# Modulation panels moved in a three-part block kernel, gated heads between output gate tiles, and two norms from one pass

## What is computed

```python
mod = silu(c) @ w_mod + b_mod                      # six vectors of 1024
h   = rmsnorm(x, g_mix) * (1 + mod[1]) + mod[0]
p   = h @ w_in                                     # forget gates, values, q, og, u, v, ga, gb
o_a = rmsnorm(hgrn2(p), g_norm_a) * silu(og)       # gated recurrence, both directions, from ctx states
o_b = gelu(u) * (w_s @ layernorm(gelu(v)) + b_s)   # spatial gate
x   = x + mod[2] * ((sigmoid(ga) * (o_a @ w_pa) + sigmoid(gb) * (o_b @ w_pb)) @ w_o)
x   = x + mod[5] * swiglu(rmsnorm(x, g_ffn) * (1 + mod[4]) + mod[3], w_up, w_down)
x   = rmsnorm(x, g_final)
```

```python
h = rmsnorm(x, g) * (1 + sc1) + sh1
y = gla_mixer(h) if l == 0 else sliding_window_attention(h, k_sh, v_sh)
x = x + g1 * y
x = x + g2 * peer(rmsnorm(x, g) * (1 + sc2) + sh2)
# after layer 0: kv_mod = silu(c_2) @ kv_mod_w + b (1024 x 2048), and from it k_sh, v_sh
# gla: 4 heads, per chunk of 64: scores, o = scores @ v + q @ state, state = a * state + k^T v
#      o = rmsnorm(o, norm_g) * silu(og); y = o @ w_out
```

## Time and profile before

| | us |
|---|---|
| median of 3 runs | 2865.52 (2862.91 to 2867.98) |
| the profiled execution | 2864.8 |
| its span in the profile | 2863.0 |
| PE busy | 2658.2 (93%) |
| DVE busy | 1691.4 (59%) |
| ACT busy | 1144.8 (40%) |
| mean granted clock of PE | 0.946 of full |

### The profile page before, as it was taken

One profiled execution on the slowest core, in us unless ns is written; L12 is line 12 of the kernel. 1 busy time (PEld: TensorE's weight loads), 2 busy tenths in 40 slices (PEclk: granted clock), 3 DMA queues, 4 the chain that ended last, 5 costly groups with the idle time before them and its releaser, 6 DMA issues.

```text
span 2863.0 us, 40826 instructions
## 1 busy us (share of the span) xinstructions
PE 2658.2 (93%) x15044; PEld 2294.9 (80%) x15044; DVE 1691.4 (59%) x3438; ACT 1144.8 (40%) x2334; POOL 3.5 (0%) x10
## 2 busy tenths in 40 slices
PE   8999999987879899999999995878899999999997
PEld 4688878645768899999888884647899999988886
DVE  3753245415538996777555556242797778655554
ACT  2412010002111356776455452232155877555454
POOL 0000000000000000000000000000000000000000
PEclk9999999997989899999999996858999999999999
DMA  6552457734615454444555555302255444455553
GB/s 244 205 202 103 144 189 276 272 117 165 248 46 189 150 184 162 141 140 142 179 196 194 191 190 196 103 0 88 90 185 183 137 145 136 161 195 196 193 190 117
DMA packets 65342, 471.55 MB, mean 165 GB/s; under 512 B 7296, under 2 KB 7552, under 8 KB 8240
## 3 DMA queue, kind: packets, MB, share of 16 engines
q1 hardware_dynamic: 64656, 467.85, 46.6%
q10 hardware_dynamic: 272, 1.05, 0.1%
q0 software_dynamic: 272, 0.69, 0.1%
HBM read 468.51 MB, written 1.05 MB: 164 GB/s over the span
## 4 chain that ended last, share of the span: by engine, by line
PE 83%; DVE 12%; DMA 2%; ACT 1%; issue 1%; SPq 0%; DVEq 0%
PE bank L633 25%; PE bank L679 24%; PE bank L481 14%; PE bank L645 4%; DVE macc L1366 3%; PE bank L723 3%; PE bank L803 2%; PE bank L491 2%; PE bank L465 2%; DMA ring<-in_w_up 1%; PE bank L406 1%; PE bank L497 1%; DVE macc L1337 1%; PE bank L721 1%; DVE arena L1482 0%
## 5 line engine op out<-in xcount | busy, mean ns | idle before, releaser
L633 PE MATMUL bank<-h_split,t_split 128*128 128x256 f32 x6144 | 777.8, 286 | 13.9 <-DVE t_split L1564 13.9
L633 PEld LDWEIGHTS bank<-h_split,t_split 128*128 128x128 f32 x6144 | 752.1, 193 | 15.6 <-DVE t_split L1564 14.7
L1564 DVE TENSOR_TENSOR t_split<-ring,t_split 128x1024 fp32r<-128x1024 f32 x512 | 625.0, 1222 | 172.7 <-ACT t_split L990 170.6
L679 PE MATMUL bank<-t_split,w_split 128*128 128x512 f32 x3072 | 698.5, 390 | 3.6 <-ACT w_split L1063 3.6
L679 PEld LDWEIGHTS bank<-t_split,w_split 128*128 128x128 f32 x3072 | 577.6, 188 | 124.1 <-ACT t_split L1061 4.0
L1061 ACT ACTIVATE t_split<-ring 128x1024 fp32r<-128x1024 f32 x256 | 271.5, 1061 | 343.8 <-PE bank L679 260.9
L990 ACT ACTIVATE t_split<-ring 128x1024 fp32r<-128x1024 f32 x256 | 270.7, 1058 | 315.4 <-PE bank L633 282.8
L481 PE MATMUL bank<-H,ring 128*128 128x256 f32 (+1 forms) x1280 | 323.4, 415 | 22.8 <-ACT H L933 11.9
L481 PEld LDWEIGHTS bank<-H,ring 128*128 128x128 f32 x1280 | 250.9, 197 | 88.0 <-issue 44.6
L1631 DVE TENSOR_TENSOR w_split<-arena,w_split 128x256 fp32r<-128x256 f32 x256 | 108.9, 425 | 296.2 <-ACT w_split L1063 296.2
L923 ACT ACTIVATE arena<-bank 128x256 f32<-128x256 f32 (+2 forms) x160 | 64.4, 406 | 533.9 <-PE bank L481 390.6
(11 more groups left out here) (258 smaller groups left out, 2202.4 us busy)
## 6 DMA issues: line engine op xcount, KB each, us to landing
ring<-in_peer_u SPq DMA_DIRECT2D x128, 1024.0 KB, 4.9
ring<-in_peer_v SPq DMA_DIRECT2D x128, 1024.0 KB, 4.9
ring<-in_mod_w SPq DMA_DIRECT2D x48, 1024.0 KB, 5.0
ring<-in_w_mod SPq DMA_DIRECT2D x24, 1024.0 KB, 5.0
ring<-in_w_in SPq DMA_DIRECT2D x22, 1024.0 KB, 5.0
ring<-in_w_up SPq DMA_DIRECT2D x22, 1024.0 KB, 5.0
ring<-in_peer_wq SPq DMA_DIRECT2D x16, 1024.0 KB, 4.9
ring<-in_w_down SPq DMA_DIRECT2D x11, 1024.0 KB, 4.9
```

Source lines behind the costliest of these rows:

```text
L633: last = mm(bank[:, 0:T], u[:, a_, k, :], h_split[:, b_, k, :], start=(k == 0 and a_ + b_ == 0), stop=(k == KT - 1 and a_ == 1))
L679: last = mm(BK[2 * tt + hf][:, :], w_split[:, j, a_, tt * P:(tt + 1) * P], t_split[:, j, b_, hf * 512:(hf + 1) * 512], start=(first and a_ ...
L1564: TT(t_split[:, j, 1, :].rearrange("p (k c) -> p k c", k=KT), ring[:, r, :].rearrange(view, k=KT, j=2)[:, j], t_split[:, j, 0, :].rearrang ...
```

## The change

- Eight of mod_w0's 24 panels go beside the last two w_in panels, the four w_pab panels and the first two w_o panels; 16 stay beside w_up (two or one per step, `UP_MODS`), none beside w_down.
- The eight kv_mod panels go beside gla_qk and gla_v (one each); their result is kept in `kvm`. `mod_stage` is gone.
- mod_w1's 24 panels go into the first peer block's V phase: one per four blocks from block 16 on, loaded into the part of `arena` whose hidden values have been used, a quarter of a sum (two operations) behind each block's splits; PE's turn stands behind the second block of four.
- The gla mixer's eight output gate tiles stand between the steps of its recurrence (four) and behind its squares (four). The gate is multiplied in first, block by block, and then the root; gla_out starts as the blocks come (`o_done` counts them).
- The end of the first block, rmsnorm(x, g_final), and the next norm of its result come from one pass: ACT squares x and g_final * x, PE sums both, and the second norm's root is that of mean((g_final x)^2) + EPS * (mean(x^2) + EPS). The normed h is made first, x itself after it.
- ACT squares a tile for a norm as soon as its residual is done, for all norms behind a residual.

The core of the diff:

```diff
+        UP_MODS = [2 if n % 2 == 0 and n < 10 else 1 for n in range(FT // 2)]
+        V_MODS, V_FROM = 24, 4
...
-                    + [(a["w_in"], 12, "proj", 2), (a["w_pab"], 4, "proj", 4), (a["w_o"], 4, "proj", 2)]
-                    + [(a["w_up"], 2, "proj", 2), (a["mod_w0"], 2, "mod_acc", 1)] * (FT // 2)
-                    + [(a["w_down"], 1, "rows", 1), (a["mod_w0"], 2, "mod_acc", 1), (a["w_down"], 10, "rows", 1),
-                     ]
-                    + [(a["gla_qk"], 1, "proj", 2), (a["mod_w1"], 2, "mod_acc", 1)] * 4
-                    + [(a["gla_v"], 1, "proj", 2), (a["mod_w1"], 1, "mod_acc", 1)] * 4
-                    + [(a["gla_og"], 1, "proj", 2), (a["mod_w1"], 1, "mod_acc", 1)] * 4
-                    + [(a["gla_out"], 4, "proj", 2)]
+                    + [(a["w_in"], 10, "proj", 2)]
+                    + [(a["w_in"], 1, "proj", 2), (a["mod_w0"], 1, "mod_acc", 1)] * 2
+                    + [(a["w_pab"], 1, "proj", 4), (a["mod_w0"], 1, "mod_acc", 1)] * 4
+                    + [(a["w_o"], 1, "proj", 2), (a["mod_w0"], 1, "mod_acc", 1)] * 2
+                    + [(a["w_o"], 2, "proj", 2)]
+                    + [x for n in range(FT // 2) for x in ((a["w_up"], 2, "proj", 2), (a["mod_w0"], UP_MODS[n], "mod_acc", 1))]
+                    + [(a["w_down"], FT // 2, "rows", 1)]
+                    + [(a["gla_qk"], 1, "proj", 2), (a["kv_mod"], 1, "mod_acc", 1)] * 4
+                    + [(a["gla_v"], 1, "proj", 2), (a["kv_mod"], 1, "mod_acc", 1)] * 4
+                    + [(a["gla_og"], 4, "proj", 2), (a["gla_out"], 4, "proj", 2)]
...
+                    with sync.Fori(0, V_MODS // 2 - 1) as i:
+                        for r in range(2):
+                            v_pairs(i * 2 + (done + r))
+                            sync.wait_ge(sems["mod_acc"], i * 2 + (total["mod_acc"] + r + 1))
+                            v_mod(i * 2 + (r + 2), r)
...
+                            for j in range(4):
+                                value_rows(j % 2, False, False)
+                                if j == 1:
+                                    pe.wait_ge(sems["mod_acc"], e.more("mod_acc"))
+                                    for x in range(2):
+                                        last = mm(BK[6][:, bass.ds(i * 4 + (2 * r + x), 1)], macc[:, r, x * P:(x + 1) * P], ones[:, 0:1],
+                                                  start=True, stop=True)
+                                    last.then_inc(sems["mod_turn"], 1)
...
+            lin_turns(M3, 0, 1)
+            lin_scores(M3, 0, 1)
+            og_tiles(1)
+            mod_between(0)
+            pe.wait_ge(sems["mod_bank"], 4)
+            lin_states(M3, 0, 1, 2, v3, 1)
+            for h in range(HEADS):
+                if h + 1 < HEADS:
+                    lin_turns(M3, h + 1, 1)
+                    lin_scores(M3, h + 1, 1)
+                    if h < 2:
+                        og_tiles(1)
+                    lin_states(M3, h + 1, 1, 2, v3, 1 if h < 2 else 0)
+                lin_out(M3, h, 1, 2, v3, None)
+            og_tiles(1)
+            lin_squares(M3, 2)
+            og_tiles(4)
+            proj_cols(4, lambda k: o8[:, k, :], T, first=True, name="o_done")
...
             for k in range(KT):
                 bank, free = ring_tile("proj")
                 TT(mg[:, k, :], bank[:, 0:T], ctxT[:, k, :], MUL).then_inc(free, 1)
+                if k % 4 == 3:
+                    used(1)
+                    mod_between(1, 16)
...
+            residual("proj", 16, (1, 3))
...
+                for b in range(4):
+                    if b % 2 == 0:
+                        dve.wait_ge(sems[f"o_bank{b // 2}"], 3)
+                    gate_block(b)
+                roots(root_buf, dv)
+                for b in range(8):
+                    if b >= 4:
+                        dve.wait_ge(sems["dve_step"], gate_block(b))
+                    TT(oT[:, b, :], oT[:, b, :], root_buf[:, b // 2 * T:(b // 2 + 1) * T], MUL).then_inc(sems["o_done"], 1)
...
+                    with dve.Fori(0, V_MODS // 2) as i:
+                        for r in range(2):
+                            for b in range(4):
+                                value_lo(b, i * 8 + (4 * V_FROM + 4 * r + b))
+                                value_mod(r, b)
...
+            def squares(src, dst, name):
                 for k in range(KT):
+                    if name:
+                        e.tiles(name, 1)
+                        act.wait_ge(*e.tile_out())
                     A(dst[:, k, :], src[:, k, :], ACT.Square).then_inc(sems["sq"], 1)
...
+                mm(BK[7][:, 0:T], ones, hT[:, k, :], start=(k == 0), stop=(k == KT - 1))
+                last = mm(BK[3][:, 0:T], ones, hT2[:, k, :], start=(k == 0), stop=(k == KT - 1))
...
+            TS(nrm[:, 0, :], BK[7][:, 0:T], 1.0 / D, EPS, MUL, ADD).then_inc(sems["dve_step"], 1)
+            STT(nrm[:, 1, :], nrm[:, 0, :], float(EPS * D), BK[3][:, 0:T], MUL, ADD).then_inc(sems["var"], 1)
```

More of the change, by code:

```diff
@@ L466, in norm, with fresh, proj_cols @@
                 last.then_inc(sems["ms"], 1)
-            def fresh(k, blocks=1):
-                pe.wait_ge(sems["h"], e.more("h", blocks))
-            def proj_cols(panels, rhs, width, ks=KT, tiles=2, cols=P, first=False):
+            def fresh(k, blocks=1, name="h"):
+                pe.wait_ge(sems[name], e.more(name, blocks))
+            def proj_cols(panels, rhs, width, ks=KT, tiles=2, cols=P, first=False, name="h"):
                 for n in range(panels):
@@ L1200, in _ @@
             rows_out(FT // 2, M2["yN"].rearrange("p (a d) -> p a d", a=2))
-            residual("turn")
-            norm(xT, hT, None)
-            act.wait_ge(sems["h"], 4 * KT)
-            norm(xT, hT, 0)
+            for k in range(KT):
+                e.tiles("turn", 1)
+                act.wait_ge(*e.tile_out())
+                A(hT[:, k, :], xT[:, k, :], ACT.Square)
+                A(hT2[:, k, :], xT[:, k, :], ACT.Square, scale=V("g_final")[:, k:k + 1]).then_inc(sems["sq"], 1)
+            act.wait_ge(sems["var"], e.more("var"))
+            A(nrm[:, 1, :], nrm[:, 1, :], ACT.Sqrt, scale=1.0 / D).then_inc(sems["std"], 1)
+            A(nrm[:, 0, :], nrm[:, 0, :], ACT.Sqrt).then_inc(sems["xstd"], 1)
+            for k in range(KT):
+                act.wait_ge(sems["hs"], e.more("hs"))
+                A(hT[:, k, :], hT[:, k, :], ACT.Identity, bias=modc[:, k:k + 1]).then_inc(sems["h"], 1)
             evac_gl = 4 + e.tile % 2
@@ L1799, in _ @@
             e.tiles("proj", 4)
+            used(10)
+            for _ in range(2):
+                used(1)
+                mod_between(1, 16)
             mg, sgb = kt(M1["fg0"], 8), Hc
@@ L1858, in _ @@
             TT(M3["kd0"], M3["kd0"], M3["k"], MUL).then_inc(sems["lin_in"], 1)
-            e.tiles("turn", 4)
-            lin(M3, 1, 2, V("gla_norm_g"), M3["zA"], 2 * P, lambda d, h: None)
+            for n in range(4):
+                used(1)
+                mod_between(1, 16)
+            mod_out(0, 16, V("kv_mod_b"), dst=kvm)
+            used(4)
+            e.tiles("proj", 8)
+            og_out = []
+            for turns, tiles in ((1, 1), (1, 1), (1, 1), (1, 1), (0, 4)):
+                e.tiles("turn", turns)
+                for _ in range(tiles):
+                    e.tiles("proj", 1)
+                    og_out.append(e.tile_out())
+            lin(M3, 1, 2, M3["zA"], 2 * P, lambda d, h: None, gated)
             residual("proj", 16)
```

370 lines of the change are left out of this document (202 added, 168 removed).

## The result

The changed kernel took 2749.6 us (median of 4 runs, 2746.4 to 2752.5) against 2865.8 for the kernel before: a ratio of 0.9595 (0.9578 to 0.9612), 116 us less. Run a second time, beside the first experiments, it took 2745.8 (5 runs), ratio 0.9578 (0.9565 to 0.9591). The forecast was 2764 with a range from 2750 to 2800: the direction and most of the size came as worked out, and the time lies just under the low end. Two executions stand apart, one of six of the kernel with fillings in the attention (4650.2 us at a mean clock of 0.681) and one of eleven of the kernel before, run beside it (3810.8 us at 0.656), and the medians and ratios given are those of the others. The question of the rest of this text is where the 15 us came from that the sum of parts doesn't have.

A forecast was written before the change was run, and what follows sets the result against it. PE, busy 93% of the span, was taken as the bound, so only its idle time, low-clock time and instructions count. Nine terms summed to -101.1 us: span 2761.9, forecast 2764 us against the median, range 2750 to 2800.

The forecast's parts named there:

- Part 1: Eight mod_w0 panels moved into the first block's output stages: PE stalls there, +3.5 us (0 to +7).
- Rival D: Covers of Part 1 and Part 6 fail (late banks, late gla_og loads): 15 to 25 us less gain, 2785; chance 0.10.
- Part 2: w_up and w_down with fewer panels between: PE's waits for queued loads go, -9.2 us (-5 to -9.2).
- Part 3: Squares behind each residual tile: PE's wait of 1.03 us goes at four places, -4.1 us (-3 to -5).
- Part 4: Two norms from one pass, ahead of the low-rank gate: PE starts earlier, -8.0 us (-5.5 to -8.6).
- Parts 5 and 7: gla_qk and gla_v with one panel each, -19.2 us; queries of the first peer block without panels, -9.0 us.
- Part 6: Gated recurrence between output gate tiles, exponents early: 84.6 to 51.6 us, 2.0 in gla_out, -35.0 (-10 to -37).
- Part 8: 24 panels into the first peer block's V phase: turns +9.7, loads 3 us, +12.7 us (+9.7 to +65).
- A: V phase bound by its loads, a value load waiting for a whole panel: 52 us more, 2816; chance 0.10.
- C: DVE bounds the V phase, kernel slower: 96 x (x - 2.82) us for x us per block; chance 0.02.
- Part 9: Behind the first V phase: eight panels and their turns gone ahead of the norm, -32.8 us (-32 to -35).
- the clock theory: Posed for the experiments: the missing 12 to 15 us are PE time at low clock that each long wait drags behind.

The follow-up runs named there:

- The long waits: Changed kernel with four waits of PE put into w_down for two DVE reciprocals each, 3.73 us of idle each: 2776.4 us, w_down 103.1 for 78.4.
- the filled ones: The same four waits in w_down of the changed kernel, with PE doing 16 matmuls of constants in each: 2760.0 us, w_down 94.0.
- the run with the parts undone: Changed kernel with 24 mod_w0 panels beside w_up and w_down again, none beside w_in, w_pab and w_o: 2756.7 us, ratio 0.9616.
- part 3 undone: Changed kernel with ScalarE waiting for all eight tiles before the first square, at all six places behind a residual: 2762.7 us.
- the last kernel: Changed kernel plus sums in parts and fillings behind norms, in the attention, at turns, first U blocks and the last norm: 2712.5 us, ratio 0.9470.

## Why the prediction was right and where it failed

**Bound.** That only PE's idle time, its time at the low clock and its instructions count was right: 80.6 us of idle time, 33.3 of faster work, and no instruction less.

**Part 1** held to 0.2 us; three stalls of two banks against a sum of 3.95 us came at the tiles that the working names, 3.0 us for 3.5. That the fourth wait brings the sum to 3.7 is luck: it was there before, and longer. Rival D's sign, a wait over 1.5 us there, didn't come: the longest is 1.32.

**Part 2 failed**, and with it the range's low end. The step is "-9.2 (-5 to -9.2)": the waits of the earlier trace rows at their bare length, as the most that could be gained. Measured net of turns 12.6, so 3.4 more. In the trace of before 64 matmuls took 1.5 us too long behind the wait of 2.10 and 1.8 behind the wait of 4.10; I read the waits and not the length of what follows them (the first 5 us behind the longer one had a mean clock of 0.66). The rest of the 3.4 is made of small pieces of both signs: the first 128 matmuls of w_up took 29.55 us before and 30.70 after. The long waits (5.3 to 6.5 us for each of 3.7) and the filled ones (3.9) show the cause in w_down, and the run with the parts undone brings both slow rows back.

**Part 3** had the direct wait right (1.03 in the brackets, 1.2 and more from start to start), and left out what is slow behind it: the queries behind the swa_out norm took 17.09 us before, 15.74 now, and 16.94 with part 3 undone.

**Part 4** came out under its own low end too (-10.5 against -8.6): 11.0 us for the 32 matmuls, from the lower clock of the earlier trace rows (0.54 in the row of 6.74 us), and they took 8.8, at 0.80. That is 2.2 of the 2.5 us of difference. Nothing waits in front of them any more; with a wait of 1.42 us put back (part 3 undone) they took 9.7.

**Parts 5 and 7** held to 0.3 us.

**Part 6**: 51.6 against 49.5. The covers held: no wait over 0.84 us between the tiles, 1.1 us in all. The 18.1 us that I took for the recurrence at full clock can't be read apart from the tiles; with the gate tiles first it took 20.6, 4.0 of it waits, which the higher clock didn't shorten: such a wait inside a head is 0.40 us in the kernel before at a clock of 0.50, and 0.84 at 1.00. Of gla_out I had 2.0 and it gave 2.4. The reason that I gave for a high clock, the tiles between, turned out not to be needed.

**Part 8**: the 9.7 for the turns against 10.4 in all. Of the 3 us that I took for the loads 0.7 was there in this trace, 2.3 in the second one. Rivals A and C were each told wrong in a detail: A's price is 0.55 us a round, not 2.3, even with a third more loads, and C's edge shows itself through late loads and costs more than its price says.

**Part 9**: 13.6 us from the turns to the next projection, 1 less than summed; the norm took 5.2 us where I had 6.0.

**The range.** Term by term the misses were -3.4 (part 2), -2.5 (4), -2.5 (6 with gla_out), -2.3 (8), -1.0 (9) and -1.3 in stages without a term, and nearly nothing the other way. Those that rows tie to the pace of matmuls behind a wait are 3.3 of part 2, 2.2 of part 4, 0.4 of gla_out and 0.8 of part 9: 6.7 of the 12.8 us between the sum and the span. So the clock theory explains about half; the reserve for loads in part 8 and some 2 us in part 6 are sizes of their own. The bounds of the parts, each taken at its low end, would have given 2750 too, but I had put the forecast's own edge at 2752 as if misses would cancel. That the time lies 0.4 us under the range and not in it is chance: the first four executions spread from 2746.4 to 2752.5. The five later ones, 2745.0 to 2747.3, all lie under it.

## What to carry to other kernels

A long wait of PE had two lengths here: the one in brackets, and what the matmuls behind it took over their normal time (0 behind 0.48 us, 1.6 to 2.8 us behind 3.73; behind 2.90 us 0 in one execution and 3.0 in another); read both rows before pricing it, and give a range of many such terms a common lean. Where a wait couldn't be removed, a few matmuls of constants into a free bank kept the clock: 16 of them in w_down's waits of 3.7 us left 1.00 behind them for 0.50 to 0.67. What a filling costs that outlasts its wait is not shown. All fillings together gave some 28 us of the last kernel's gain (an estimate: 33 to 37 less the 6.6 of the sums in parts), more than most of the reorderings. And the sums that take DVE away for 3.95 us each cost the two stages that hold them 6.6 us less, cut in parts between tiles or moved ahead of a wait.

## What the runs showed of the hardware that was not expected

- The same wait of 2.90 us was followed once by 3.7 and once by 6.7 us for the same 16 matmuls, in two executions of one program; that is where its times from 2745 to 2752 come from in part.
- The attention, with waits of only 1.09 us in each 5.15, stood at half the clock for 70 us and more, while the recurrence with waits of 0.8 us in each 4.95 stood at full clock. One came into its stretch behind long waits (4.29 and 2.67 us) and the other behind 28 us of tiles (clock 1.00). But the recurrence before the change also came in behind a long wait, and recovered after 18 us. Why the attention doesn't recover by itself stays open; that filling lifts it is shown (0.96 for 0.50).
- At 352 GB/s (0.91 of the DMA engines' time) value loads of 1 MB still landed in 5.0 us by the median, while one issued right behind another took 8.5.
